# Three parts per feed-forward, and nine gate-and-up jobs of the last one as seven block products

## The reference

```python
# ffn0, in the first block
gt, up = jnp.split(jnp.einsum("bsd,df->bsf", h, w_ffn_up[l]), 2, axis=-1)
x = x + g2 * jnp.einsum("bsf,fd->bsd", jax.nn.silu(gt) * up, w_ffn_down[l])

# ffn1 and ffn2, in the second block
def conv_glu_ffn(h, w_up, conv_w, conv_b, w_down):
    a, b = jnp.split(h @ w_up, 2, axis=-1)
    a_pad = jnp.pad(a, ((0, 0), (CONV_WIDTH_2 - 1, 0), (0, 0)))
    a = sum(conv_w[j] * a_pad[:, j:j + S] for j in range(CONV_WIDTH_2)) + conv_b
    return (jax.nn.silu(a) * b) @ w_down
```

## Time and profile before

| | us |
|---|---|
| median of 3 runs | 2094.66 (2092.9 to 2097.76) |
| the profiled execution | 2093.53 |
| its span, first to last instruction | 2091.7 |
| PE busy | 2059.9 (98%) |
| DVE busy | 989.1 (47%) |
| ACT busy | 885.9 (42%) |
| POOL busy | 840.6 (40%) |

### The profile page before, as it was taken

How to read it: one execution, slowest core, us unless ns; L and a number is a source line. 1 busy time by engine, 2 the same in 40 slices (tenths; PEclk the granted TensorE clock), 3 DMA queues, 4 the chain that set the end, 5 groups by cost and what they waited for, 6 DMA issues and landing times.

```text
span 2091.7 us, 28578 instructions
## 1 busy us (share of the span) xinstructions
PE 2059.9 (98%) x10618; PEld 1735.8 (83%) x10618; DVE 989.1 (47%) x1909; ACT 885.9 (42%) x1307; POOL 840.6 (40%) x273
## 2 busy tenths in 40 slices
PE   9999999999999999999999999999999999999998
PEld 6888977888888888876877888888887588888887
DVE  4889788574311111376985344034323934431432
ACT  3355545463443222534366453233423954432332
POOL 3443422444244444433713443444443044444443
PEclk9999999999999999999999999999999999999999
DMA  9654322325232432432202433333422034324322
GB/s 371 243 185 125 102 62 66 101 85 178 81 100 81 114 107 78 113 93 65 79 24 64 113 100 93 107 105 94 143 86 73 2 96 121 100 80 121 100 70 91
DMA packets 304008, 220.17 MB, mean 105 GB/s; under 512 B 13520, under 2 KB 288080, under 8 KB 301616
## 3 DMA queue, kind: packets, MB, share of 16 engines
q1 hardware_dynamic: 293216, 195.67, 31.1%
q10 hardware_dynamic: 10704, 23.33, 3.7%
HBM read 213.48 MB, written 2.10 MB: 103 GB/s over the span
## 4 chain that ended last, share of the span: by engine, by line
PE 85%; DVE 7%; issue 3%; ACT 2%; POOL 2%; DMA 0%; ACTq 0%; DVEq 0%; SPq 0%; POOLq 0%
PE bank L912 72%; PE bank L1159 2%; PE bank L1375 2%; PE bank L1353 2%; DVE arena L2811 1%; PE bank L1307 1%; DVE small L2809 1%; PE bank L1362 1%; PE bank L1458 1%; PE bank L1207 1%; POOL w_split_out L2851 1%; DVE bank L2277 1%; POOL w_split L2851 1%; PE bank L1218 1%; PE bank L1540 1%
## 5 line engine op out<-in xcount | busy, mean ns | idle before, releaser
L912 PE MATMUL bank<-h_hi,w_split 128*128 128x512 f32 x3696 | 1119.4, 382 | 1.8 <-DVE arena L2679 1.1
L2851 POOL TENSOR_TENSOR w_split<-wslots,w_split 128x2048 fp32r<-128x2048 f32 (+3 forms) x174 | 712.7, 4097 | 987.9 <-ACT w_split L1613 549.5
L912 PEld LDWEIGHTS bank<-h_hi,w_split 128*128 128x128 f32 x3696 | 698.7, 189 | 116.8 <-issue 15.7
L912 PE MATMUL bank<-h_lo,w_split 128*128 128x512 f32 x1848 | 701.8, 380 | 0.0
L912 PEld LDWEIGHTS bank<-h_lo,w_split 128*128 128x128 f32 x1848 | 349.7, 189 | 51.2 <-issue 3.4
L912 PE MATMUL bank<-hid_hi,w_split 128*128 128x512 f32 x1056 | 316.2, 380 | 2.2 <-DVEq L2562 2.2
L1634 ACT ACTIVATE w_split<-wslots 128x2048 fp32r<-128x2048 f32 (+2 forms) x80 | 141.4, 1767 | 368.0 <-PE bank L912 368.0
L1613 ACT ACTIVATE w_split<-wslots 128x2048 fp32r<-128x2048 f32 (+3 forms) x91 | 158.8, 1745 | 300.8 <-PE bank L912 278.9
L912 PEld LDWEIGHTS bank<-hid_hi,w_split 128*128 128x128 f32 x1056 | 199.6, 189 | 32.3 <-issue 3.6
L912 PE MATMUL bank<-hid_lo,w_split 128*128 128x512 f32 x528 | 200.1, 379 | 0.0
L2277 DVE SCALAR_TENSOR_TENSOR bank<-arena,cols,bank 128x512 f32<-128x512 f32 x240 | 161.3, 750 | 5.4 <-ACT bank L1727 4.9
(11 more groups left out here) (341 smaller groups left out, 2352.4 us busy)
## 6 DMA issues: line engine op xcount, KB each, us to landing
wslots<-in_f_w_up SPq DMA_DIRECT2D x88, 512.0 KB, 4.7
wslots<-in_w_in SPq DMA_DIRECT2D x24, 1024.0 KB, 5.3
wslots<-in_w_ffn_up SPq DMA_DIRECT2D x44, 512.0 KB, 4.5
arena<-in_w_ada ACTq DMA_DIRECT2D x8, 2048.0 KB, 9.1
wslots<-in_f_w_down SPq DMA_DIRECT2D x16, 768.0 KB, 4.8
wslots<-in_a_w_in SPq DMA_DIRECT2D x10, 1024.0 KB, 5.2
wslots<-in_f_w_down SPq DMA_DIRECT2D x16, 640.0 KB, 4.4
arena<-in_w_ada_first SPq DMA_DIRECT2D x8, 1024.0 KB, 19.3
```

What stands on the lines that cost most here:

```text
L912: return nc.tensor.matmul(bank[:], w, woven(x), start=start, stop=stop)
L2851: last = nc.gpsimd.tensor_tensor(part[:, 1, cols_of], slot(p, 1, size)[:, 0, cols_of], part[:, 0, cols_of].bitcast(F32), ALU.subtract)
```

## The change

Three things change together. (1) `PARTS` replaces `HALVES` in all three feed-forwards: 8, 8 and 6 hidden tiles, so three up stages and three down stages instead of two and two. (2) `first_downs` serves every down stage of the three, and computes all tiles but the last of job 0, then of job 1, then the two last tiles; job 1 uses bank 2p + 1 beside job 0's bank 2p, where p is job 0's slot, and no longer waits for its own slot's banks. (3) In ffn2 nine up jobs (jobs 4 and 6 of part 0, jobs 0, 2, 4 and 6 of part 1, jobs 0, 2 and 4 of part 2; always the even ones) become "units": the 1024 x 256 weights are a 2 x 2 array of blocks, and so is h (two halves of features by two halves of tokens), and the product is made of seven block products instead of eight, each 4 x 3 matmuls with 256 columns. For that DVE makes four sums of weight blocks for each unit (128 x 512) and once four sums of token blocks (128 x 1024), ACT makes the upper parts, POOL the lower parts, and DVE adds the products to the four results (`early_sums`, `late_sums`). The weights of an odd job are split in two halves of 1024 columns.

Left out of the diff below: the layout of memory and constants, the counts of semaphores, semaphores that are renamed or shared.

```diff
-HALVES = ((0, 12), (12, FT - 12))
+PARTS = ((0, 8), (8, 8), (16, FT - 16))
+LAST = len(PARTS) - 1
+SEVEN = (2,)
+def seven_at(k, part, i):
+    return k in SEVEN and (0 if part else 2) <= i < PARTS[part][1] // 2
...
 # PE, first_downs
-                for j, (q, first, end) in enumerate(((p, 0, kc - 1), (other, 0, 3), (p, kc - 1, kc), (other, 3, kc))):
-                    if j < 2:
-                        start_split(name, j)
-                    tiles(q, first, end)
+                start_split(name, 0)
+                tiles(p, 0, kc - 1)
+                pe.wait_ge(lo_ready[other], SPLITS_BEFORE[FIRST[name] + 1] + 1)
+                tiles(other, 0, kc - 1)
+                tiles(p, kc - 1, kc)
+                tiles(other, kc - 1, kc)
...
+            def seven_products(k, part, i):
+                name, unit = f"ffn{k}_up{part}", (k, part, i)
+                q, use = one(name, 2 * i)
+                pe.wait_ge(bank_free[q], use + 1)
+                for e, bank, at, tokens in ((0, 7, 0, 2), (1, 7, 1, 0), (2, 6, 1, 1), (4, 6, 0, (0, 0)), (3, 2 * q, 1, (1, 1)), (5, 2 * q, 0, (1, 0)), (6, 2 * q + 1, 0, 3)):
+                    if e < 6:
+                        pe.wait_ge(S["sums_lower"], LOWER[unit] + e + 1)
+                    else:
+                        pe.wait_ge(lo_ready[q], SPLITS_BEFORE[FIRST[name] + 2 * i] + 1)
+                    for c in range(DT // 2):
+                        for wp, hp in ((0, 0), (0, 1), (1, 0)):
...
+                    if e in (3, 4):
+                        last.then_inc(S["g_turned_then_products"], 1)
+                last.then_inc(product_done[q], 1)
...
             def ffn(k):
-                for half, (t0, n) in enumerate(HALVES):
...
+                for part, (t0, n) in enumerate(PARTS):
+                    up_part(k, part)
+                    first_downs(f"ffn{k}_down{part}", n, lambda c, half: hid[half][:, c, :], ("hid_ready", 2 + FT * k + t0))
...
 # ACT, ffn
+                if k and k in SEVEN:
+                    for c in range(DT):
+                        last = nc.scalar.activation(tokens_of(c), token_rows(xT[:, c, :]), ACT.Copy, scale=late_gain(f"ffn{k}", c))
...
+                        if i == 0 and seven_at(k, part, 0):
+                            first_product(k, part, 0)
+                        if following:
+                            sum_uppers(*following)
+                            block_uppers(*following)
+                        else:
+                            split_job(slot_after(FIRST[name] + 2 * i))
+                        conv_or_gate(2 * i, p, use)
+                        gate_and_upper(2 * i, p)
+                        if i == part == 0 and k in SEVEN:
+                            token_upper(k, 2)
+                            token_upper(k, 0)
...
+                    if part < LAST:
+                        for j in range(DT):
+                            n = slot_after(FIRST[down] + j)
+                            if seven_at(k, part + 1, 0) and n == FIRST[f"ffn{k}_up{part + 1}"]:
+                                sum_uppers(k, part + 1, 0)
+                                block_uppers(k, part + 1, 0)
+                            else:
+                                split_job(n)
...
 # DVE
+            def token_sums_made(k):
+                def sum_of(j, a, b):
+                    nc.vector.tensor_tensor(token_plain[j], token_plain[a], token_plain[b], ALU.subtract).then_inc(S["angle_then_sum_ready"], 1)
...
+            def three_sums(k, part, i):
+                n = FIRST[f"ffn{k}_up{part}"] + 2 * i
+                dve.wait_ge(weights_in[n % 2], LOADED[n])
+                before = UNITS.index((k, part, i)) - 1
+                if before >= 0:
+                    dve.wait_ge(S["g_turned_then_products"], PRODUCTS[UNITS[before]] + 1)
+                sum_of_blocks(k, 0, block_of(k, 0, 0), block_of(k, 1, 0), ALU.subtract)
+                sum_of_blocks(k, 1, block_of(k, 1, 0), block_of(k, 1, 1), ALU.add)
+                dve.wait_ge(S["angle_then_sum_ready"], SUMS[k, part, i] + 2)
+                sum_of_blocks(k, 2, entry_sums[k][1], block_of(k, 0, 0), ALU.subtract)
+            def fourth_sum(k, part, i):
+                dve.wait_ge(S["angle_then_sum_ready"], SUMS[k, part, i] + 3)
+                sum_of_blocks(k, 3, block_of(k, 0, 1), entry_sums[k][2], ALU.subtract)
...
+            def up_part(k, part, turn):
+                name, tiles = f"ffn{k}_up{part}", PARTS[part][1]
+                for i in range(tiles // 2):
+                    following = (k, part, i + 1) if seven_at(k, part, i + 1) else None
+                    unit = seven_at(k, part, i)
+                    if unit and i == 0:
+                        early_sums(k, part, 0)
+                    if following:
+                        three_sums(*following)
...
+                        fourth_sum(*following)
+                    if unit:
+                        late_sums(k, part, i)
+                    turn(2 * i, None)
+                    turn(2 * i + 1, (lambda: early_sums(*following)) if following else None)
...
             def ffn(k):
-                for half, (t0, tiles) in enumerate(HALVES):
+                if k in SEVEN:
+                    token_sums_made(k)
+                for part, (t0, tiles) in enumerate(PARTS):
...
 # POOL, ffn
+                        if seven_at(k, part, i):
+                            entry_lowers(k, part, i)
+                        else:
+                            lower_job(f"ffn{k}_up{part}", 2 * i)
+                        if part == 0 and i == 1 and k in SEVEN:
+                            token_lower(k, 2)
+                            token_lower(k, 0)
+                        if i:
+                            lower_in_halves(k, part, i)
+                        else:
+                            lower_job(f"ffn{k}_up{part}", 1)
```

More of the change, by code:

```diff
@@ new lines, in sum_counts @@
+def sum_counts():
+    n, at = 4, {}
+    for k in SEVEN:
+        at[k] = n
+        n += 4
+        for part, (_, tiles) in enumerate(PARTS):
+            for i in range(-1, tiles // 2):
+                if seven_at(k, part, i + 1) and (i >= 0 or part):
+                    at[k, part, i + 1] = n
+                    n += 4
+                if seven_at(k, part, i) and k == 0:
+                    n += 1
+                    at[k, part, i, "late"] = n
+    return at
+UPPER, SUMS = upper_counts(), sum_counts()
@@ L413, in build, with block_of @@
         SIZE["a_uk"] = SIZE["a_uv"] = 2 * D
-        SIZE |= {f"ffn{k}_{what}{half}": n for k in range(3) for half, (_, tiles) in enumerate(HALVES)
+        SIZE |= {f"ffn{k}_{what}{part}": n for k in range(3) for part, (_, tiles) in enumerate(PARTS)
                 for what, n in (("up", DT * 2 * P), ("down", tiles * P))}
+        def block_of(k, m, half):
+            return slot(FF_PARITY[k], DT, 2 * P)[:, DT // 2 * half:DT // 2 * (half + 1), m * P:(m + 1) * P]
         def pairs(eng, name, first=0, end=None):
@@ L1567, in idle_products @@
                 for _ in range(n):
-                    nc.tensor.matmul(banks[7][:], con("one"), trig[:, 0, :], start=True, stop=True)
+                    nc.tensor.matmul(banks[7][:], con("one"), wslots[:, 0:T], start=True, stop=True)
             before = TILES_BEFORE["last"]
@@ L1945, in take, with gate_and_upper @@
+                            return
+                        if t % 2 == 0 and seven_at(k, part, t // 2):
+                            act.wait_ge(S["angle_then_sum_ready"], SUMS[k, part, t // 2, "late"])
+                        nc.scalar.activation(halves(up_gate[:, p, :]), plain(banks[2 * p][:]), ACT.Silu).then_inc(S["act_gate"], 1)
+                    def gate_and_upper(t, p, first=None):
+                        n = FT * k + t0 + t
+                        if k:
                             act.wait_ge(S["conv3_ready"], n - FT + 1)
-                            gates = halves(up_acc[:, p, :])
@@ new lines, in late_sums @@
+            def late_sums(k, part, i):
+                q, use = one(f"ffn{k}_up{part}", 2 * i)
+                first, sums = up_gate[:, 1 - q, :], up_gate[:, q, :]
+                gates, ups = banks[2 * q], banks[2 * q + 1]
+                dve.wait_ge(product_done[q], use + 1)
+                steps.settle()
+                steps.did(nc.vector.tensor_tensor(gates[:, LOW], gates[:, LOW], first[:, LOW], ALU.add))
+                steps.did(nc.vector.tensor_tensor(gates[:, HIGH], gates[:, HIGH], sums[:, HIGH], ALU.add))
+                steps.did(nc.vector.tensor_tensor(ups[:, LOW], ups[:, LOW], sums[:, LOW], ALU.add))
+                last = nc.vector.tensor_tensor(ups[:, HIGH], banks[7][:, HIGH], sums[:, LOW], ALU.add)
+                if k:
+                    steps.did(last)
+                else:
+                    last.then_inc(S["angle_then_sum_ready"], 1)
+                    dve.wait_ge(S["angle_then_sum_ready"], SUMS[k, part, i, "late"])
+                steps.settle()
@@ L2752, in ffn, with turn @@
```

(5 more changed lines are left out.)

348 lines of the change are left out of this document (268 added, 80 removed).

## The result

The changed kernel takes 2167.24 us (median of 4 runs, 2161.99 to 2168.61) against 2095.97 before: ratio 1.0337, 95% interval 1.0315 to 1.0359. It is 71 us slower; 2158 was forecast, in a range of 2122 to 2178. The profiled execution took 2166.61, its span is 2164.8, 73.1 more than before.

What follows compares the result with a forecast made beforehand. The prediction took PE's own work plus each hole in it as the bound. Ten terms, savings -8.8 and -2.6 against added holes and clock, summed to +63.8 on 2093.53, giving 2157.3, as median 2158 (range 2122 to 2178).

Steps and rivals of the forecast that it cites:

- third down job: Down stages: weights wait for job 0's last tile, one tile covers 3.88 of preparation; holes of 3.2 or 2.5, +22.3.
- down to up: First up job after a down stage in ffn0 and ffn1: weights 1.8 late with restart, four times, +7.2.
- ffn0's last stage: Six-tile down stage: DVE's serial turn of 4.5 exceeds PE's job of 3.89 and becomes the bound, +8.5.
- ffn1's last stage: Six-tile down stage: third job's hole 3.1, and late b_q weights hold up ACT and b_mem's bank by 5.6; +8.7.
- ffn2's start: DVE's token and first unit sums, blocked by POOL's subtractions, free PE's banks late: holes of 7.6 and 4.5, +12.1.
- unit to unit: Between units in ffn2: DVE's chain ends at 20.1, PE wants the banks at 19.74; four times, +2.0.
- part that begins with a unit: ffn2, twice: late weights for the next unit make banks ready at 23.5 for 19.74, +7.6.
- clock: PE's clock falls after one in three of twelve new holes of 2.5 or longer, 1.7 each, +6.8.
- The one with a free port: Rival: shared SBUF access does not block DVE's sums, or they slip between POOL's subtractions; 2142, chance 0.18.
- The one in which transfers land late as well: Rival: the clock falls after nearly every hole (+20 for 6.8) and late transfers add some 3; 2174, chance 0.10.
- The covers: Rival: ACT and POOL prepare the third job and first up job in time, only savings stay; 2083, chance 0.06.
- the matmuls of 256 columns: Rival: in units a short matmul waits for its weight load, 0.19 instead of 0.11; near 2217, chance 0.03.

Runs made afterwards that it cites:

- three_tiles: Changed kernel, but only three tiles of job 1, not all but its last, come before job 0's last tile in `first_downs`: 2142.12 us (1.0217).
- six_first: Changed kernel with ffn0 and ffn1 in parts of 6, 8 and 8 tiles, ffn2 unchanged: 2160.68 us (1.0306).
- act_order: Changed kernel, but in ffn1's last down stage ACT copies b_q's first weights behind its work for down job 6: 2159.25 us (1.0295).
- pool_waits: Changed kernel, but POOL begins its subtraction for ffn2's job 2 only after DVE's four token sums: 2164.94 us.
- no_head_units: Changed kernel, but parts 1 and 2 of ffn2 begin with an ordinary job, so two units fewer: 2159.5 us (1.0306).
- thirds_tuned: Changed kernel with ffn0/ffn1 in halves, three tiles of job 1 between, POOL waiting for token sums, no units heading parts 1 and 2: 2101.44 us (1.003).
- parts_only: Changed kernel without any units (no block products), three parts and new tile order kept: 2159.38 us (1.0312).
- sums_later: Changed kernel, but in ffn2 DVE makes the four token sums behind its turn for job 0, not ahead: 2171.32 us (1.0361).

## Why the prediction was right, and where it was off

Each term against the profiled execution. Holes are here PE's start-to-start distances less the spacing, so they are some 0.15 longer than the waits of the view. A "restart" is the matmul behind a hole, whose distance to the next is 0.1 longer than the spacing, or 0.34 to 0.37 where the clock is already low (at third down jobs what is above 0.1 is counted with the clock).

| term | forecast | measured |
|---|---|---|
| 9 units (9.37 for 10.36) | -8.8 | -8.9 |
| last hidden tile | -2.6 | -3.0 |
| third down job: 6 x 3.22, 2.42, restarts 0.7 | +22.3 | +22.4 |
| down to up: 1.68 to 1.70, four times, restarts | +7.2 | +7.1 |
| ffn0's last stage | +8.5 | +9.0 |
| ffn1's last stage: 3.08, 5.46, restarts | +8.7 | +9.0 |
| ffn2's start: 6.93, 2.58, restarts | +12.1 | +10.0 |
| unit to unit | +2.0 | 0 |
| part that begins with a unit: 3.1, 4.1, restarts | +7.6 | +8.1 |
| clock | +6.8 | +18 |
| sum | +63.8 | +72 |

Of the remaining 1 of the 73.1, 0.7 lies in PE's first 25 us, which the change does not touch.

The forecast came out 9.3 below the profiled execution, and part of its closeness is luck: the clock was put 11 too low, and the holes, taken together, 3 too high.

- **The holes.** Eight terms without the clock and the units were forecast at +65.8 and measured at +62.6. The third job's (3.2 from ACT 1.06, POOL 2.36 and 0.46 against one tile) was right in every stage, and `three_tiles` showed the mechanism: more cover, smaller hole. `six_first` showed that of ffn0's last stage, `act_order` that of ffn1's, `pool_waits` the blocked sum.
- **ffn2's start**, 2.1 too high, 1.9 of it in its second hole, 2.6 for 4.5. The four sums meet POOL's subtractions as forecast (10.1 from 1816.64 to 1826.69), and the banks come 31.3 behind the start of job 0's turn where the working had 32.3. The rest is the clock: it fell in the first hole and brought PE to the second 1.5 later, while DVE, ACT and POOL kept their pace. Eight kernels begin ffn2 this way. In the 5 us behind the first hole PE lost 5 x (1 - granted clock), and the second wait is shorter by as much; in the changed kernel, `three_tiles` and `no_head_units` it is 2.42, 2.05 and 2.57 behind

```profile
1809.53:1814.53 5.00, 5.00 (x15) 4.11 (x16) 2.82 (x5) 4.16 (x6) 4.91 (x3) 0.64 0.01 3
...
1793.31:1798.31 5.00, 5.00 (x13) 4.05 (x14) 2.83 (x5) 4.15 (x6) 4.91 (x3) 0.56 0.01 3
...
1814.68:1819.68 5.00, 5.00 (x15) 4.15 (x16) 2.83 (x5) 4.16 (x6) 4.90 (x3) 0.66 0.01 3
```

The loss and the wait together are 4.2 to 4.3 in all eight, also in the two whose first wait is 2.5 and not 6.8 (`pool_waits`, `thirds_tuned`). So what the clock takes from PE ahead of a longer hole costs nothing: a slow PE hides part of the next hole.
- **Unit to unit.** The working had the even job's chain end at 20.1 where PE comes at 19.74. In the trace the fourth sum of a unit that starts at 1943.98 begins 10.2 behind it and takes 1.58, `late_sums` ends at 13.1 for 13.6, and the chain ends just in time. A difference of 0.4 between two sums of ten terms was no ground for a hole.
- **The clock** is the step that was mis-sized: "a fall after one in three". Of 15 holes of 2.3 or longer 11 had a stretch at the lower level in them or behind them, most at a cost of 1.5 to 1.7, some 2.8 at 639.98 and 2.6 at 2074.11: 19.9 in all, and before's own at 905 did not come (-1.7). Over the changed kernel and the five variants with its parts and order of tiles, 27 of the 36 holes of 3.2 at third down jobs were followed by a fall (`six_first` adds 3 of 4), and none of the 32 of 1.7 at first up jobs (those of `three_tiles` counted too). The price of one fall, 1.7, was about right. The frequency could not be had from the earlier trace rows, one fall and none, and these were no pair: the wait at 1061.75, behind which the clock stayed up, was 2.25, longer than the 1.58. With 11 falls in place of 4 the sum of the prediction would have been 2170.
- **Length alone does not decide.** Where PE turns from full work to attention b's first, small score products (L1489, a wait of 1.8 to 1.9) the clock fell in 9 of the 12 kernels, though in none of the 32 of 1.7 behind which PE went on with full jobs. In `parts_only`:

```profile
1654.20:1657.60 3.40, 3.40 (x11) 1.37 (x10) 1.44 (x9) 1.78 (x8) 0.00 (x0) 0.50 0.00 0
```

- **Sums of the working.** By its own terms fourteen new holes are 2.5 or longer, not twelve, which at one in three is +7.9 for +6.8. The upper bounds of the terms add up to +80, 2175, not +82 and 2177. Both are small beside the range.
- **The rivals.** The one with a free port is out by the 5.47. The one in which transfers land late as well named the right cause for the rest: it had +20 for the clock, and its 2174 is nearer to the measured 2167 than the forecast's 2158; only its late transfers did not come. The covers did not hold, and the matmuls of 256 columns ran at 0.1117 each.

## What to carry to other kernels

A shorter stage is not a smaller copy of a longer one: all that is prepared behind a job's back (the weights of the job after next, the late norm, the next transfer) keeps its length while its cover shrinks, so write down for each preparation what covers it, in us, before and after. A saving on the bounding engine of 1 us in 10 is spent by a single hole, and of the holes of 2.3 us or longer in the changed kernel 11 of 15 cost some 1.7 more through the clock. When a producer is moved, move its consumers in the other engines' lists too.

## What the runs showed of the hardware

- A hole of 3.2 in PE's work was followed by a stretch at the lower clock in 27 of 36 cases, a hole of 1.7 at the first up job in 0 of 32, a wait of 1.8 to 1.9 ahead of attention b's small score products in 9 of 12, and behind the same hole, where two kernels are the same up to it, the clock fell in one and not in the other (not at 1428.55 of the changed kernel, but at 1429.78 in `sums_later`, at 0.50 for 3.5 us). Runs of one changed kernel differ by 10 us where the kernel before has 6, and their mean granted clocks differ with them (0.987 and 0.991 for 9.4 us in `parts_only`).
- A DVE sum of 128 x 1024 with both operands in SBUF took 1.23 alone and 5.47 when POOL's subtraction had begun 0.67 before it; sums of 512 columns among POOL's subtractions took 1.58 or 2.7 for 0.69.
- A lower granted clock of PE did not slow the others: in the 5 us behind ffn2's first hole DVE, ACT and POOL were busy 2.8, 4.2 and 4.9 at a granted clock of 0.56 as at 0.66, and PE's loss and the wait that followed came to 4.2 to 4.3 in eight kernels.
